# Waits on the operation read, and the decoding of the choice moved between the next round's maxima

## The reference, cut to what matters

```python
s1 = jnp.einsum('nhd,hkd->nhk', q1, sub_k1)       # 128 scores
s2 = jnp.einsum('nhd,hkd->nhk', q2, sub_k2)       # 128 scores
v1, i1 = lax.top_k(s1, 16)
v2, i2 = lax.top_k(s2, 16)
cand = (v1[..., :, None] + v2[..., None, :]).reshape(n, 8, 256)
top_s, top_c = lax.top_k(cand, 16)
e1 = jnp.take_along_axis(i1, top_c // 16, axis=-1)
e2 = jnp.take_along_axis(i2, top_c % 16, axis=-1)
idx = e1 * 128 + e2
g = jax.nn.softmax(top_s, axis=-1)
```

## Time and profile before

| what | us |
|---|---|
| median of 3 runs (lowest, highest) | 2630.54 (2628.7, 2637.44) |
| profiled execution, its own time | 2631.61 |
| its span | 2629.8 |
| DVE busy in the span | 2203.7 (84%) |
| PE busy in the span | 2457.1 (93%) |
| ACT busy in the span | 1097.8 (42%) |
| POOL busy in the span | 1360.0 (52%) |

### The profile page before, as it was taken

How to read it: one execution, slowest core, us unless ns; L and a number is a source line. 1 busy time by engine, 2 the same in 40 slices (tenths; PEclk the granted TensorE clock), 3 DMA queues, 4 the chain that set the end, 5 groups by cost and what they waited for, 6 DMA issues and landing times.

```text
span 2629.8 us, 38758 instructions
## 1 busy us (share of the span) xinstructions
PE 2457.1 (93%) x13131; PEld 2079.6 (79%) x13131; DVE 2203.7 (84%) x3953; ACT 1097.8 (42%) x1938; POOL 1360.0 (52%) x1054
## 2 busy tenths in 40 slices
PE   7989999899999999999986878999999999999997
PEld 5767888788876788878865667888988898988886
DVE  6355445886779897877899988999999999999999
ACT  4463444333257323333316993333333333343333
POOL 0000000315732555645754447888878877778885
PEclk9999999999999999999998999999999999999999
DMA  6735545457963897977942459999999999999997
GB/s 246 274 127 178 193 142 190 161 202 271 389 239 113 307 333 266 352 253 265 383 123 106 193 224 391 410 405 415 415 415 411 415 414 415 415 415 396 415 414 286
DMA packets 240278, 787.50 MB, mean 299 GB/s; under 512 B 21888, under 2 KB 75184, under 8 KB 219408
## 3 DMA queue, kind: packets, MB, share of 16 engines
q0 software_dynamic: 112288, 408.77, 39.8%
q1 hardware_dynamic: 127856, 377.00, 38.4%
HBM read 728.01 MB, written 57.67 MB: 299 GB/s over the span
## 4 chain that ended last, share of the span: by engine, by line
PE 38%; DVE 28%; issue 17%; DMA 8%; ACT 6%; POOL 3%; DVEq 0%; POOLq 0%; SPq 0%; ACTq 0%
PE lin L245 10%; PE lin L247 10%; PE lin L246 10%; DVE Y L2360 3%; DVE row_ring L138 2%; DMA rows<-in_up,now 2%; DVE w_lo L222 2%; DMA w_raw<-in_wall 2%; DVE rows L2347 2%; DVE w_raw L2347 2%; DMA G<-in_downT 2%; DVE low L2333 2%; DVE low L2338 2%; ACT row_ring L1811 1%; ACT w_hi L214 1%
## 5 line engine op out<-in xcount | busy, mean ns | idle before, releaser
L150 POOL DMA_INDIRECT row_ring<-in_down,IDX x256 | 359.4, 1404 | 316.5 <-DVE dots L138 243.3
L222 DVE TENSOR_TENSOR w_lo<-w_raw,w_hi 128x2048 fp32r<-128x2048 f32 x100 | 230.1, 2301 | 234.9 <-ACT w_hi L214 225.0
L245 PE MATMUL lin<-w_hi,T_hi 128*128 128x512 f32 x976 | 389.1, 399 | 15.9 <-DVE w_lo L222 7.9
L247 PE MATMUL lin<-w_hi,T_lo 128*128 128x512 f32 x976 | 388.6, 398 | 0.0
L246 PE MATMUL lin<-w_lo,T_hi 128*128 128x512 f32 x976 | 386.4, 396 | 0.0
L214 ACT ACTIVATE w_hi<-w_raw 128x2048 fp32r<-128x2048 f32 x116 | 221.9, 1914 | 364.3 <-PE lin L247 342.1
L2237 POOL DMA_INDIRECT rows<-in_up,now x192 | 311.3, 1621 | 66.0 <-issue 54.9
L245 PE MATMUL lin<-w_hi,c_hi 128*128 128x512 f32 x768 | 307.6, 401 | 20.9 <-DVE c_lo L2373 20.9
L138 DVE CUSTOM_DVE_ANT_0 row_ring<-row_ring,H 128x1024 f32<-128x1024 f32 x256 | 306.8, 1237 | 24.0 <-DMA row_ring<-in_down,IDX 23.2
L2237 POOL DMA_INDIRECT w_raw<-in_up,now x192 | 281.9, 1468 | 85.2 <-issue 43.0
L245 PE MATMUL tr<-T_hi,w_hi 128*128 128x384 f32 x896 | 304.4, 340 | 3.1 <-DVE low L2333 3.1
(11 more groups left out here) (296 smaller groups left out, 5263.9 us busy)
## 6 DMA issues: line engine op xcount, KB each, us to landing
w_raw<-in_wall SPq DMA_DIRECT2D x116, 1024.0 KB
row_ring<-in_up SPq DMA_DIRECT2D x128, 512.0 KB
G<-in_downT SPq DMA_DIRECT2D x112, 512.0 KB
wd<-dense_gates SPq DMA_DIRECT2D x32, 768.0 KB
weight_rests<-w_lo SPq DMA_DIRECT2D x16, 1024.0 KB, 5.1
w_lo<-weight_rests SPq DMA_DIRECT2D x16, 1024.0 KB, 4.9
dense_gates<-peer SPq DMA_DIRECT2D x6, 2048.0 KB, 7.2
dense_gates<-w_raw SPq DMA_DIRECT2D x6, 2048.0 KB, 6.3
```

The costliest lines, as they stand in the source:

```text
L150: pool.indirect_dma_start(self.ring[:, r % self.K, :], None, self.table, bass.IndirectOffsetOnAxis(ap=self.IDX[:, r:r + 1], axis=0)).then_ ...
L222: dve.tensor_tensor(self.lo[:, h % 2], self.raw[:, h % 2], self.hi[:, h % 2].bitcast(F32), ALU.subtract).then_inc(self.lo_done, 1)
L245: pe.matmul(out, lhs[0], rhs[0], start=start, stop=False, skip_group_check=True)
L247: return pe.matmul(out, lhs[1], rhs[0], start=False, stop=stop, skip_group_check=True)
```

## The change

- `link` is gone from the rounds of the sample (it stays in `shift` and `finish`). `counted` lets every maximum, cut and decoding step count `chain`, and `after(n)` lets an instruction wait only until the count has passed the one that it reads.
- `decode(u)` is a generator: round r steps it once after each first maximum, so the six decoding steps of unit r-2 stand between the six maxima of round r.
- `look(u)`, the comparison of unit r-2, stands behind the first pair of index and cut of round r. DVE no longer waits for `marked`.
- POOL's look-up in step r is that of unit r-2 (before: r-1). There is a step and a round more (`UNITS + 1`); that last round holds only decoding and comparison of unit 15, behind `shift(3)` and ahead of the last stamp.
- The last `aside()` of a round is no longer inside the condition `r >= 1`, so round 0 takes one gathered row more.

```diff
+            def after(n):
+                dve.wait_ge(chain, n)
+            def counted(instruction):
+                nonlocal links
+                instruction.then_inc(chain, 1)
+                links += 1
+                return links
+            def decode(u):
+                a_, b_ = part_b[:, :, 0, :], part_b[:, :, 1, :]
+                skip = SPLIT - WIDE * WIDE
+                after(picked[u])
+                counted(dve.tensor_scalar(shifted[:, 0], pos[:], 4, None, ALU.logical_shift_right))
+                yield
+                n = counted(dve.tensor_scalar(shifted[:, 1], pos[:], 2, None, ALU.logical_shift_right))
+                yield
+                after(n)
+                n = counted(dve.scalar_tensor_tensor(out=a_, in0=shifted[:, 1], scalar=float(-skip // WIDE),
+                                                     in1=shifted[:, 0], op0=ALU.add, op1=ALU.max))
+                yield
...
+            def look(u):
+                if u == 0:
+                    dve.wait_ge(tables_done, 1)
+                if u >= 2:
+                    dve.wait_ge(looked_up, u - 1)
+                after(decoded[u])
+                dve.tensor_tensor(pick[:, u % 2], part_b[:].rearrange("p h s j -> p (h s j)").unsqueeze(1).broadcast_to(
+                    (P, TOPK, LOOK)), place[:], ALU.is_equal).then_inc(marked, 1)
...
+                steps = decode(r - 2) if r >= 2 else iter(())
+                first, cut, second = {}, {}, {}
                 for n, (v, i, src, rest) in enumerate(rows):
                     if n == ones:
                         dve.wait_ge(paired, r)
-                    last = dve.max(v[:, 0:8], src)
+                    first[n] = counted(dve.max(v[:, 0:8], src))
+                    next(steps, None)
+                for _ in steps:
+                    pass
                 aside()
-                link(last)
                 for n, (v, i, src, rest) in enumerate(rows):
+                    after(first[n])
+                    if n == ones and r >= 2:
+                        after(decoded[r - 2])
                     dve.max_index(i[:, 0:8], v[:, 0:8], src)
-                    last = dve.match_replace(rest, v[:, 0:8], src, LOWEST)
+                    cut[n] = counted(dve.match_replace(rest, v[:, 0:8], src, LOWEST))
+                    if n == 0 and r >= 2:
+                        look(r - 2)
                     if n == 2:
                         aside()
...
@@
             shift(3)
+            pick_experts(UNITS + 1)
             while stamps < ND * OCTS:
                 stamp()
@@
-            for r in range(UNITS + 1):
+            for r in range(UNITS + 2):
@@
-                u = r - 1
+                u = r - 2
                 if u >= 0:
                     pool.wait_ge(marked, u + 1)
```

More of the change, by code:

```diff
@@ L1892, in _ @@
             dve.tensor_tensor(H[:, NG - 1, :], G[:, GATHERED, :], row, ALU.mult).then_inc(h_done, 1)
+            def after(n):
[17 more added lines that the diff above has]
+                yield
+                after(n)
+                n = counted(dve.tensor_scalar(start[:], a_, float(WIDE), float(skip), ALU.mult, ALU.add))
+                yield
+                after(n)
+                n = counted(dve.scalar_tensor_tensor(out=start[:], in0=a_, scalar=float(TOPK), in1=start[:],
+                                                     op0=ALU.mult, op1=ALU.min))
+                yield
+                after(n)
+                n = counted(dve.scalar_tensor_tensor(out=b_, in0=pos[:], scalar=0.0, in1=start[:], op0=ALU.add,
+                                                     op1=ALU.subtract))
+                decoded[u] = n
+                yield
+            def look(u):
[6 more added lines that the diff above has]
+                    (P, TOPK, LOOK)), place[:], ALU.is_equal).then_inc(marked, 1)
+            picked, decoded = {}, {}
             def pick_experts(r, aside=lambda: None):
@@ L1907, in pick_experts @@
                 ones = len(rows)
[L1908 removed]
+                if 1 <= r <= UNITS:
                     c, t = order[r - 1]
@@ L1914, in pick_experts @@
                         dve.wait_ge(paired, r)
-                    last = dve.max(v[:, 0:8], src)
+                    first[n] = counted(dve.max(v[:, 0:8], src))
+                    next(steps, None)
+                for _ in steps:
+                    pass
                 aside()
-                link(last)
                 for n, (v, i, src, rest) in enumerate(rows):
+                    after(first[n])
+                    if n == ones and r >= 2:
+                        after(decoded[r - 2])
                     dve.max_index(i[:, 0:8], v[:, 0:8], src)
-                    last = dve.match_replace(rest, v[:, 0:8], src, LOWEST)
+                    cut[n] = counted(dve.match_replace(rest, v[:, 0:8], src, LOWEST))
+                    if n == 0 and r >= 2:
+                        look(r - 2)
                     if n == 2:
                         aside()
+                if not rows:
+                    look(r - 2)
                 aside()
-                link(last)
-                for v, i, src, rest in rows:
-                    last = dve.max(v[:, 8:16], rest)
+                for n, (v, i, src, rest) in enumerate(rows):
+                    after(cut[n])
+                    second[n] = counted(dve.max(v[:, 8:16], rest))
                 aside()
-                link(last)
                 for n, (v, i, src, rest) in enumerate(rows):
+                    after(second[n])
                     last = dve.max_index(i[:, 8:16], v[:, 8:16], rest)
@@ L1934, in pick_experts @@
                 if len(rows) > ones:
[L1935 to L1938, removed]
[L1941 to L1960 removed]
+                    picked[r - 1] = counted(last)
+                aside()
             def shift(i):
```

14 lines of the change are left out of this document (removed).

## The result

The changed kernel takes **2645.29 us** (median of 7 runs, 2642.63 to 2653.62) against 2630.54 of the kernel before on the same chip: ratio 1.0062, 95% interval 1.0048 to 1.0075. A second measurement gave a ratio of 1.0058 (1.0035 to 1.0080). It is slower by 0.6%, as forecast (2642, range 2625 to 2655). The profiled execution is a long one, the longest of the seven, 2653.62 us with a span of 2651.8.

What follows compares the result with a forecast made beforehand. DVE's chain of waits was taken to bound the kernel from round 3, ACT's from 1509.8 us. Terms: +4 to the first stamp, +8 in stamp rounds, -1 at the end: +11 us, so 2642, range 2625 to 2655.

Steps and rivals of the forecast that it cites:

- The sign and the mechanism: Slower, about +11 us in all: beside POOL's look-up, DVE's decoding steps are held for up to a whole POOL instruction.
- A plain round: A round without stamps: 8.1 us unhindered plus 3.1 held makes 11.2, against 9.5 today.
- step 3: Third of DVE's six decoding steps in a plain round: waits for the end of POOL's product, at +3.0 us.
- steps 5 and 6: Last two decoding steps in a plain round: wait for the first two of POOL's sums, split as 1.15 and 0.67 us.
- Rounds 3 and 4 and the sums between them: Round 3 without a look-up beside its steps -1.4 us, the two sums -1.2, round 4 held +1.7.
- Round 8 and the first stamp: Round 8, its shift falling into the same hold, -0.2 us; first stamp, waiting for unit 6's look-up, +0.9.
- The stamp rounds: From the first stamp on: held steps add 1.1 us in each of seven transitions, +8, less 1 at the end.
- the first of my two cases: Stamp rounds: POOL gets in only at a stamp's end and holds the steps 3.35 us, round 21.8.
- Nothing meets: Rival: steps slip between POOL's instructions or POOL waits; plain rounds 8.1 to 8.6 us, total 2620; chance 0.15.
- Only shifts and comparison: Rival: of DVE's steps only these are held; plain rounds 8.1 + 1.0 us, total 2632; chance 0.25.
- Everything held: Rival: comparison held too; plain rounds 11.7 us, stamp rounds 22.8, total 2650; chance 0.15, shared with waits not free.
- Waits not free: Rival: some 30 waits and counts a round cost 1.2 us a round, 10 at most; chance within 0.15 for everything held.

Runs made afterwards that it cites:

- experiments 3 to 5: POOL's product and three sums removed from the changed kernel (2610.9 us) and from the kernel before (2615.9); then only the sums removed from the changed kernel (2618.4).
- 1: Changed kernel with its single waits kept, but decoding, comparison and POOL's look-up back where they stood before the change: 2628.6 us, ratio 0.9986.
- 2: Changed kernel with the steps still between the maxima, but each phase again waiting for the last operation of the one before: 2652.0 us, ratio 1.0072.
- experiment 5: Changed kernel without POOL's three sums, its product and last addition kept: plain round 9.94 us, median 2618.4 us in one run.
- Experiment 10: Changed kernel with POOL's look-up ahead of the candidates only from step 15 on: 2643.6 us in one run.
- experiment 6: Changed kernel with POOL's look-up ahead of the candidates instead of behind them: 2617.1 us, ratio 0.9929; again 2618.7 us, ratio 0.9941.

## Why the prediction was right, and where not

**The sign and the mechanism** stand. The steps are held by POOL's product and sums (experiments 3 to 5), in plain and in stamp rounds alike. The comparison takes 0.67 to 0.69 in all 16 rounds, but it never ran beside POOL's product or sums, so no run shows whether it can be held. The waits aren't what costs (1, 2). ACT's waits grew from 7.4 to 12.6 where I said some 15. Of the six steps three take the 0.5 to 2 us that I named as the sign; the others take 0.22, 0.41 and 0.27. The total's closeness is in part luck: single terms miss by up to 3.4 us, in both directions.

**A plain round:** 11.59 for 11.2. Unhindered I had 8.1; the run without the look-up's work has 8.22. The holds are 3.4, not 3.1. I let step 3 wait for the product and steps 5 and 6 for the first two sums, and took L1919, step 4, for free, since it has one input. In the run it is the second shift that waits for the product, and steps 3, 4 and 5 wait for the three sums: L1919 is held by a sum like its neighbours, 0.61 for 0.16. The Trainium skill (VectorE: DVE Perf Modes, section "Mode 2×_2P — use both read ports for one tensor") says that an operation with a single source in SBUF can use both read ports of the engine. Such an operation contends with GpSimd by the section of the Trainium skill that the prediction cites (SBUF — State Buffer, "Who interferes with whom"), and that makes L1919 one of those that contend. The trace agrees: 0.61 beside a sum, 0.15 with the sums taken away (experiment 5).

**Rounds 3 and 4 and the sums between them:** here the terms were -1.4, -1.2 and +1.7, the measured +0.79 and -1.34; together -0.9 predicted and -0.55 measured. These are the two largest misses, +3.4 and -3.0, and that they cancel is luck. The two sums do fall from 5.14 to 4.28, but DVE now comes to them early and waits for PE, which I had left out. Round 3's own -1.4 is there, the sums give 0.9, and the wait takes 3.06 back. It is a term with a wide spread: in the ten profiles with the steps between the first maxima DVE waits there for 0 to 5.1 us.

```profile
1338.66 4.28 DVE L2043 TENSOR_TENSOR ahead<-T_hi,T_lo 128x1536 f32<-128x1536 f32 x2 [3.06 <-PE lin L247]
```

And round 4 isn't held, since these sums keep DVE (until 1342.94) until POOL's look-up is all but over (1343.60). So of four rounds that I counted as held three are: 3 x 2.07 = 6.2 for 6.8 - 1.7 = 5.1.

**Round 8 and the first stamp, where the sum itself was wrong:** +0.7 predicted, +3.0 measured, and nothing cancels it. Each of the two terms is nearly right by itself: from `halved` to the stamp 7.44 for 7.06, +0.4 where I said +0.9; from the start of round 8 to that of `finish(0)` 11.91 for 11.54, +0.4 where I said -0.2. But I had measured round 8 from start to start and the stamp from `halved`. Before, the steps stand behind `halved`; in the changed kernel, held, they stand ahead of it. From the start of round 8 to its `halved` it is 8.89 before and 11.50 after, +2.6, and my -0.2 was for the whole round, whose part behind `halved` the stamp's term counts once more. When a change moves work across the point from which the next stage is reckoned, the sum has to be cut at that point. The wait itself is as predicted: the first stamp stands behind ACT's copy.

```profile
1404.72 1.22 DVE L2027 TENSOR_TENSOR w_hi<-keys,pairs 128x1024 fp32r<-128x1024 f32 x1 [0.86 <-ACT pairs L1827]
```

**The stamp rounds:** +1.1 in each of seven and -1 at the end were predicted, 7; measured +6.1, again with two errors that cancel by luck: +4.0 for 8 up to unit 15's candidates, +2.15 for -1 behind them. Rounds without a shift or finish beside them grew by 0.9 to 1.1 (20.98 to 21.98, 21.05 to 21.97, 20.96 to 22.09). They are near the first of my two cases (21.8): POOL gets in at a stamp's end, and product and sums then hold the steps, in round 11 from 1444.39 us on for 1.91, 1.17, 0.61 and 0.41. Those with a shift or finish grew by 0.2 or fell by 0.15; that these go into the same hold, as in round 8, is my reading and no run takes it apart. And the last round, of which I said that it adds nothing, adds: round 16 meets two look-ups, unit 13's behind step 15's candidates and unit 14's behind its own comparison. The stamps of the second one keep ACT waiting:

```profile
1562.65 1.91 POOL L2117 TENSOR_TENSOR pick<-pick,id_b 128x1024 bf16<-128x1024 bf16 x1 [1.72 <-DVE pick L1937]
1562.99 2.66 DVE L2027 TENSOR_TENSOR w_hi<-keys,pairs 128x1024 fp32r<-128x1024 f32 x1
1564.65 4.45 POOL L2122 TENSOR_TENSOR pick<-pick 128x512 bf16<-128x512 bf16 x3
1565.57 1.64 DVE L2032 TENSOR_TENSOR mark<-keys_b,pairs_b 128x1024 bf16<-128x1024 bf16 x1
...
1567.24 2.45 ACT L1811 ACTIVATE row_ring<-mark,pairs 128x128 f32<-128x128 bf16 x8 [2.32 <-DVE mark L2032]
```

From unit 15's candidates to the last store it is 35.9 us, before 33.7. Experiment 10 supports this reading by 2 us, though not as cleanly as planned; how much of it is the order of the last round rather than the second look-up stays open.

**The rivals.** "Nothing meets" is out by the rows above, though its price for a plain round (8.1) is what experiment 6 gets. "Only shifts and comparison": L1915 and L1922 are held. "Everything held": the comparison met nothing here, and the plain round and the total (11.59, 2645.3) lie between the forecast and this rival (11.7, 2650); its stamp round of 22.8 is out (22.0). Whether a comparison can be held isn't tested. "Waits not free": experiment 1 shows them to be worth their joins. What stays open: why `experts` differs by 11 us between two executions of one kernel.

## What to carry to other kernels

Before moving small DVE steps to fill gaps, ask what POOL does in that stretch: a 0.16 us step costs up to the whole POOL instruction that it meets, and a row of steps with unheld operations between them met four POOL instructions in turn. The cure may lie on the other engine: an order that was harmless (POOL's look-up behind the candidates) becomes the loss when what it reads is ready a round earlier, and exchanging two blocks of POOL's program turned +0.6% into -0.6%. And cut a predicted sum at points that both kernels pass in the same order of work.

## What I had not expected of the hardware

- A DVE step with one input, bfloat16 in and fp32 out, is held by POOL's two-input sums: 0.61 for 0.16 us (L1919), and 0.15 again with the sums taken away.
- Two whole stamps, four DVE instructions one behind the other, keep POOL out: its second candidate instruction takes 3.72 us and ends 0.2 after the last of them, and the pair takes 4.08 us for 0.71. Experiment 6 has the same 3.72 in its stamp rounds; before the change it is 2.01:

```profile
1550.88 4.08 POOL L2105 TENSOR_TENSOR cand<-best 128x128 f32<-128x128 f32 x2 [13.20 <-DVE ids L1989]
1551.21 1.20 DVE L2027 TENSOR_TENSOR w_hi<-keys,pairs 128x1024 fp32r<-128x1024 f32 x1
...
1554.07 0.68 DVE L2032 TENSOR_TENSOR mark<-keys_b,pairs_b 128x1024 bf16<-128x1024 bf16 x1
```

- Two profiled executions of the changed kernel agree to 0.02 us at the last store of the choice and differ by 11 us in the 1060 behind it.
